# The first output projection of a two-layer attention kernel: ten of its sixteen strips in five pairs, each pair as seven block products

## What is computed

```python
o_mla = _mla_branch(...) * jax.nn.silu(gate_mla)     # 512 x 1024
o_fox = _fox_branch(...) * jax.nn.silu(gate_fox)     # 512 x 1024
o = jnp.concatenate([o_mla, o_fox], axis=-1) @ w_out # 512 x 2048 times 2048 x 2048
return x + _rms_norm(o, g_post)                      # what the second layer reads
```

## Time and profile before

| | |
|---|---|
| median of 3 runs | 1803.67 us |
| the profiled execution | 1803.62 us, its span 1801.8 us |
| PE busy | 1785.9 us, 99% of the span |
| DVE busy | 1043.7 us, 58% |
| ACT busy | 663.2 us, 37% |
| chain that ended last | 93% on PE |

### The profile page before, as it was taken

One profiled execution on the slowest core, in us unless ns is written; L12 is line 12 of the kernel. 1 busy time (PEld: TensorE's weight loads), 2 busy tenths in 40 slices (PEclk: granted clock), 3 DMA queues, 4 the chain that ended last, 5 costly groups with the idle time before them and its releaser, 6 DMA issues.

```text
span 1801.8 us, 24913 instructions
## 1 busy us (share of the span) xinstructions
PE 1785.9 (99%) x8748; PEld 1493.7 (83%) x8748; DVE 1043.7 (58%) x2150; ACT 663.2 (37%) x1265; POOL 49.0 (3%) x77
## 2 busy tenths in 40 slices
PE   9999999999999999999999999999999999999997
PEld 7788888888888888888878887888888888888887
DVE  7444434444433788853348865767667666784334
ACT  6433223222223444542236343434443334352222
POOL 0000000000000000000002000000000000000001
PEclk9999999999999999999999999999999999999999
DMA  6443434342232433233238364211212222223332
GB/s 238 141 124 116 130 102 119 111 120 85 85 102 71 139 106 128 94 113 102 94 97 225 105 220 142 70 58 59 81 47 83 84 68 81 75 77 129 116 122 100
DMA packets 56323, 196.46 MB, mean 109 GB/s; under 512 B 6624, under 2 KB 7800, under 8 KB 55744
## 3 DMA queue, kind: packets, MB, share of 16 engines
q1 hardware_dynamic: 49392, 170.87, 28.8%
q0 software_dynamic: 6864, 24.69, 5.3%
HBM read 187.11 MB, written 8.43 MB: 109 GB/s over the span
## 4 chain that ended last, share of the span: by engine, by line
PE 93%; DVE 4%; DVEq 1%; ACT 1%; issue 1%; DMA 0%; SPq 0%; ACTq 0%
PE strip L442 23%; PE strip L444 23%; PE strip L443 23%; PE scores L442 3%; PE scores L443 3%; PE scores L444 3%; PE outputs L444 2%; PE outputs L443 2%; PE outputs L442 2%; PE scores L484 1%; PE scores L536 1%; PE scores L544 1%; PE scores L943 1%; PE scores L540 1%; PE scores L966 1%; PE scores L902 1%
## 5 line engine op out<-in xcount | busy, mean ns | idle before, releaser
L442 PE MATMUL strip<-xh,wh 128*128 128x512 f32 (+1 forms) x1896 | 743.6, 392 | 2.5 <-DVE xl L1941 1.5
L444 PE MATMUL strip<-xh,wl 128*128 128x512 f32 (+1 forms) x1896 | 735.4, 388 | 0.0
L443 PE MATMUL strip<-xl,wh 128*128 128x512 f32 (+1 forms) x1896 | 734.8, 388 | 0.0
L1540 DVE TENSOR_TENSOR wl<-raw,wh 128x1024 fp32r<-128x1024 f32 (+3 forms) x306 | 354.7, 1176 | 141.9 <-ACT wh L1054 141.2
L442 PEld LDWEIGHTS strip<-xh,wh 128*128 128x128 f32 x1896 | 356.2, 188 | 77.3 <-DVE xl L1941 2.4
L444 PEld LDWEIGHTS strip<-xh,wl 128*128 128x128 f32 x1896 | 356.0, 188 | 74.0
L443 PEld LDWEIGHTS strip<-xl,wh 128*128 128x128 f32 x1896 | 356.4, 188 | 70.6 <-issue 0.5
L1054 ACT ACTIVATE wh<-raw 128x1024 fp32r<-128x1024 f32 (+3 forms) x308 | 305.8, 1018 | 130.7 <-PE strip L444 93.2
L1076 ACT ACTIVATE prob<-prob,nms 128x128 f32<-128x128 f32 (+3 forms) x128 | 70.3, 551 | 100.7 <-DVE nms L1595 100.7
L1326 ACT ACTIVATE e_t<-o 128x512 f32 (+1 forms) x29 | 18.3, 632 | 214.3 <-DVE o L2020 109.6
L1548 DVE TENSOR_TENSOR y<-strip,rb 128x512 f32<-128x512 f32 x47 | 32.5, 691 | 103.9 <-PE strip L444 101.7
(11 more groups left out here) (438 smaller groups left out, 2083.5 us busy)
## 6 DMA issues: line engine op xcount, KB each, us to landing
raw<-in_w SPq DMA_DIRECT2D x308, 512.0 KB, 3.5
mfox<-in_mfox POOLq DMA_DIRECT2D x8, 640.0 KB, 4.1
mfox<-decay POOLq DMA_DIRECT2D x8, 640.0 KB, 7.6
xn<-o POOLq DMA_DIRECT2D x4, 1024.0 KB, 8.0
xr<-xn POOLq DMA_DIRECT2D x16, 256.0 KB, 3.0
o<-in_xt SPq DMA_DIRECT2D x7, 512.0 KB, 9.3
out<-oh SPq DMA_DIRECT2D x14, 256.0 KB, 2.5
o<-in_xt POOLq DMA_DIRECT2D x13, 256.0 KB, 6.6
```

What stands on the lines that cost most here:

```text
L442: pe.matmul(out, ah, bh, start=first, stop=False, skip_group_check=shared)
L443: pe.matmul(out, ah, bl, start=False, stop=False, skip_group_check=shared)
L444: return pe.matmul(out, al, bh, start=False, stop=last, skip_group_check=shared)
L1540: v_.tensor_tensor(wl[s][:, :cols], raw[s][:, :cols], wh[s][:, :cols].bitcast(F32), ALU.subtract)\
```

## The change

Ten strips (6 to 15) become five pairs. A pair is a 2x2 block problem: two output strips (j, j+1) by two halves of the tokens, and each block sums over two halves of the 16 tiles. In place of 8 block products there are 7 (Winograd's form of Strassen's scheme). Each is 8 tiles x 3 matmuls of 256 columns. Four of them take sums of weight units, four take sums of activations.

Of the four units of a pair m0, m1 (strip j) and m2, m3 (strip j+1) VectorE makes four sums of 128x1024 in order: s1 = m2+m3, s2 = m0-m2, s3 = s1-m0, s4 = m1-s3. Products 0 to 6 use m0, s1, s3, m1, s2, s4, m3; each of the seven gets its `wh` on ScalarE and its `wl` on VectorE. The sums of activations are the same for all pairs: before the first pair VectorE makes three differences of 256 columns for each of 8 k and a fourth in place in `o` (`t_of`), ScalarE rounds them (`th`, 128x768), VectorE makes their remainders (`t_rest`), and the fourth is split in two instructions of 128x1024 on each engine (`last_tile`, `last_rest`).

The products go to three banks, of which each pair uses the other three: 0 and 3 to `bx`, 1 and 5 to `bz`, 2, 4 and 6 to `by`. What a bank holds in between is read out: `p1` by ScalarE, and `p15`, `p16` and three of the four quarters of the result by VectorE (256 columns each), the fourth by ScalarE. TensorE waits for `p1` ahead of product 3, for `p16` ahead of product 4, for the late half of strip j+1 ahead of product 6. The weights in HBM are the same, and four units are loaded for a pair. The loads and the memset of GpSimd move to the end of the last pair, and one unit's remainder of the next stage moves behind its fourth new tile.

```diff
+PAIRS = 5
+FEWER = 4 * PAIRS
...
-U_CMPIN = U_OUT1 + 32
+U_PAIRS = U_OUT1 + 12
+U_CMPIN = U_PAIRS + 8 * 5
...
+def conv(q, i=0):
+    return U_PAIRS + 8 * q + i
+def pair_unit(q, m):
+    return U_PAIRS + 4 * q + m
...
+    chunks = [at["rb"] + 6144 * i for i in (0, 2, 3, 4)] + [stage + 6144 * i for i in range(4)]
+    th = [place(f"th{i}", [P, 3, 256], F32R, chunks[i]) for i in range(8)]
+    tl = [place(f"tl{i}", [P, 3, 256], F32R, chunks[i] + 3072) for i in range(8)]
+    tf = [place(f"tf{i}", [P, 3, 256], offset=chunks[i] + 3072) for i in range(8)]
+    wsum = place("wsum", [P, 1024], offset=stage + 24576)
+    p1 = place("p1", [P, 256], offset=at["gate"])
+    p16 = place("p16", [P, 256], offset=at["gate"] + 1024)
+    p15 = place("p15", [P, 256], offset=at["rb"] + 30720)
...
+    def pair_banks(q):
+        return (sb[0], sb[1], sb[2]) if q % 2 == 0 else (pj[N_OUT1 % 2], pj[1 - N_OUT1 % 2], po)
+    pair_from = (raw[2], wsum, raw[2], raw[3], raw[0], wsum, raw[1])
...
+        for q_ in range(1, PAIRS):
+            for m in range(4):
+                u = pair_unit(q_, m)
+                sp.wait_ge(w_lo, conv(q_ - 1, (4, 4, 5, 8)[m]))
+                sp.dma_start(raw[u % SLOTS][:, :], d["w"][u, :, :]).then_inc(raw_full[u % SLOTS], 16)
...
-        g.wait_ge(o_done, 16)
-        g.memset(blk[:, :, :], 0.0).then_inc(blk_zero, 1)
+        g.wait_ge(w_used, conv(PAIRS - 1, 5))
         g.dma_start(xr1[:, :, :], d["xt"][:, 0:2, :]).then_inc(xr1_in, 16)
         g.dma_start(xr1c[:, :, :], d["xt"][:, 2:3, :]).then_inc(xr1c_in, 16)
         g.dma_start(cos2[:, :], d["cos_a"]).then_inc(tab2_in, 16)
         g.dma_start(sin2[:, :], d["sin_a"]).then_inc(tab2_in, 16)
+        g.wait_ge(w_used, conv(PAIRS - 1, 6))
+        g.memset(blk[:, :, :], 0.0).then_inc(blk_zero, 1)
...
-        with pe.Fori(1, KT // 2 - 1) as i:
-            for s in range(4):
-                half(pe, At(U_OUT1 + 4 + s, i, 4), N_OUT1 + s // 2, s % 2, N_OUT1 + 1 + s // 2 + i * 2)
+        for s in range(4):
+            half(pe, At(U_OUT1 + 8 + s), N_OUT1 + s // 2, s % 2, N_OUT1 + 1 + s // 2)
+        def product(q, i, out, first, bh, bl):
+            pe.wait_ge(w_lo, conv(q, 8 if i == 6 else i + 1))
+            slot = conv(q, i) % SLOTS
+            for k_ in range(8):
+                cols = slice(P * k_, P * k_ + P)
+                ins = three(pe, out[:, 0:256], wh[slot][:, cols], wl[slot][:, cols], bh(k_), bl(k_),
+                            first and k_ == 0, k_ == 7, True)
+            ins.then_inc(w_used, 2 if i == 6 else 1)
+        def of_x(first, tokens):
+            return lambda k_: xh[:, first + k_, tokens], lambda k_: xl[:, first + k_, tokens]
+        def of_t(j):
+            return lambda k_: th[k_][:, j, :], lambda k_: tl[k_][:, j, :]
+        for q_ in range(PAIRS):
+            bx, bz, by = pair_banks(q_)
+            pe.wait_ge(y_done, N_OUT1 + 2 * q_ + 4)
+            product(q_, 0, bx, True, *of_x(0, TOKENS[0]))
+            if q_ == 0:
+                pe.wait_ge(t_lo, 8)
+            product(q_, 1, bz, True, *of_t(0))
+            product(q_, 2, by, True, *of_t(1))
+            pe.wait_ge(p1_out, q_ + 1)
+            product(q_, 3, bx, False, *of_x(8, TOKENS[0]))
+            pe.wait_ge(w_part, 3 * q_ + 2)
+            product(q_, 4, by, False, *of_t(2))
+            product(q_, 5, bz, False, *of_x(8, TOKENS[1]))
+            pe.wait_ge(w_part, 3 * q_ + 3)
+            if q_ == 0:
+                pe.wait_ge(t4_lo, 2)
+            product(q_, 6, by, False, *of_x(0, TOKENS[1]))
...
+        def pair_hi(q, i):
+            if q == PAIRS:
+                act_hi(a, At(U_CMPIN + i))
                 return
-            a.wait_ge(acc_ready, 3)
-            a.wait_ge(w_used, U_CMPIN)
-            a.activation(e_t[:, :], pj[1 - N_OUT1 % 2][:, :], ACT.Square).then_inc(ev_act, 1)
-
-        two_strips(At(U_CMPIN - 4), last_square, more=(6,))
+            if i in (0, 3, 6):
+                u = pair_unit(q, {0: 0, 3: 1, 6: 3}[i])
+                a.wait_ge(raw_full[u % SLOTS], (u // SLOTS + 1) * 16)
+            else:
+                a.wait_ge(s_made, 4 * q + {1: 1, 4: 2, 2: 3, 5: 4}[i])
+            a.wait_ge(w_used, conv(q, i - 3))
+            a.activation(wh[conv(q, i) % SLOTS][:, :], pair_from[i][:, :], ACT.Copy).then_inc(w_hi, 2 if i == 6 else 1)
+        def last_tile(b):
+            a.wait_ge(w_used, U_PAIRS)
+            a.activation(xh[:, 4 * b:4 * b + 4, TOKENS[1]], o[:, 8 + 4 * b:12 + 4 * b, TOKENS[0]], ACT.Copy)\
+             .then_inc(t4_hi, 1)
...
+        for i in range(3):
+            pair_hi(0, i)
+        square_of(5)
+        for q_ in range(PAIRS):
+            bx, _, _ = pair_banks(q_)
+            j = 6 + 2 * q_
+            pair_hi(q_, 3)
+            if q_ == 0:
+                last_tile(0)
+            else:
+                square_of(j - 2)
+            a.wait_ge(w_used, conv(q_, 1))
+            a.wait_ge(y_done, N_OUT1 + j)
+            a.activation(p1[:, :], bx[:, 0:256], ACT.Copy).then_inc(p1_out, 1)
+            pair_hi(q_, 4)
+            if q_ == 0:
+                last_tile(1)
+            else:
+                a.wait_ge(r_done, N_OUT1 + j - 1)
+                square_of(j - 1)
+            pair_hi(q_, 5)
+            pair_hi(q_, 6)
+            a.wait_ge(w_used, conv(q_, 4))
+            a.activation(o[:, j, TOKENS[0]], bx[:, 0:256], ACT.Copy)
+            for i in range(3 if q_ < PAIRS - 1 else 2):
+                pair_hi(q_ + 1, i)
+        a.drain()
+        square_of(KT - 2)
+        a.wait_ge(r_done, N_OUT1 + KT - 1)
+        a.activation(e_t[:, TOKENS[1]], o[:, KT - 1, TOKENS[1]], ACT.Square)
+        a.wait_ge(y_done, N_OUT1 + KT)
+        a.activation(e_t[:, TOKENS[0]], o[:, KT - 1, TOKENS[0]], ACT.Square).then_inc(ev_act, 1)
+        act_hi(a, At(U_CMPIN + 2))
...
+        def t_of(k_):
+            early, late = TOKENS
+            v_.tensor_tensor(tf[k_][:, 0, :], o[:, k_, late], o[:, k_, early], ALU.subtract)
+            v_.tensor_tensor(tf[k_][:, 2, :], o[:, 8 + k_, late], o[:, k_, late], ALU.subtract)
+            v_.drain()
+            v_.tensor_tensor(tf[k_][:, 1, :], o[:, 8 + k_, late], tf[k_][:, 0, :], ALU.subtract)
+            v_.drain()
+            v_.tensor_tensor(o[:, 8 + k_, early], o[:, 8 + k_, early], tf[k_][:, 1, :], ALU.subtract).then_inc(t_made, 1)
+        def t_rest(k_):
+            v_.wait_ge(t_hi, k_ + 1)
+            v_.tensor_tensor(tl[k_][:, :, :], tf[k_][:, :, :], th[k_][:, :, :].bitcast(F32), ALU.subtract)\
+              .then_inc(t_lo, 1)
...
+        def pair_lo(q, i):
+            if q == PAIRS:
+                lo(v_, At(U_CMPIN + i))
+                return
+            slot = conv(q, i) % SLOTS
+            v_.wait_ge(w_hi, conv(q, 8 if i == 6 else i + 1))
+            v_.tensor_tensor(wl[slot][:, :], pair_from[i][:, :], wh[slot][:, :].bitcast(F32), ALU.subtract)\
+              .then_inc(w_lo, 2 if i == 6 else 1)
+        def loaded(q, m):
+            u = pair_unit(q, m)
+            v_.wait_ge(raw_full[u % SLOTS], (u // SLOTS + 1) * 16)
+        def first_sums(q):
+            loaded(q, 2)
+            loaded(q, 3)
+            v_.tensor_tensor(wsum[:, :], raw[0][:, :], raw[1][:, :], ALU.add).then_inc(s_made, 1)
+            loaded(q, 0)
+            v_.tensor_tensor(raw[0][:, :], raw[2][:, :], raw[0][:, :], ALU.subtract).then_inc(s_made, 1)
+        def third_sum(q):
+            v_.drain()
+            v_.tensor_tensor(raw[2][:, :], wsum[:, :], raw[2][:, :], ALU.subtract).then_inc(s_made, 1)
+        def fourth_sum(q):
+            v_.drain()
+            loaded(q, 1)
+            v_.tensor_tensor(wsum[:, :], raw[3][:, :], raw[2][:, :], ALU.subtract).then_inc(s_made, 1)
+        t_of(0)
+        t_of(1)
...
+        out1(4)
+        out1_square(4)
+        t_rest(7)
+        pair_lo(0, 0)
+        first_sums(0)
+        pair_lo(0, 1)
+        third_sum(0)
+        pair_lo(0, 2)
+        fourth_sum(0)
+        out1(5)
+        out1_square(5)
+        for q_ in range(PAIRS):
+            bx, bz, by = pair_banks(q_)
+            j = 6 + 2 * q_
+            more = q_ < PAIRS - 1
+            pair_lo(q_, 3)
+            if q_ == 0:
+                last_rest(0)
+            pair_lo(q_, 4)
+            if q_ == 0:
+                last_rest(1)
+            else:
+                out1_square(j - 2)
+            v_.wait_ge(p1_out, q_ + 1)
+            v_.wait_ge(w_used, conv(q_, 2))
+            v_.tensor_tensor(p15[:, :], bz[:, 0:256], p1[:, :], ALU.add).then_inc(w_part, 1)
+            pair_lo(q_, 5)
+            if q_ > 0:
+                out1_square(j - 1)
+            v_.wait_ge(w_used, conv(q_, 3))
+            v_.tensor_tensor(p16[:, :], by[:, 0:256], p1[:, :], ALU.add).then_inc(w_part, 1)
+            pair_lo(q_, 6)
+            if more:
+                pair_lo(q_ + 1, 0)
+            v_.drain()
+            v_.wait_ge(w_used, conv(q_, 5))
```

(23 more changed lines are left out.)

130 lines of the change are left out of this document (92 added, 38 removed).

## The result

| | before | after |
|---|---|---|
| median | 1803.73 us (15 runs, 1803.16 to 1804.07) | 1807.02 us (15 runs, 1805.80 to 1808.63) |
| ratio after / before | | 1.0019, 95% interval 1.0012 to 1.0026 |
| the profiled execution | 1803.62, span 1801.8 | 1806.3, span 1804.5 |

The change costs 3.3 us, 0.19%. That is inside the range and within 0.2% of the forecast, but the forecast was +0.8. The five pairs save nothing, as predicted; some 2.5 us come on top.

What follows compares the result with a forecast made beforehand. The prediction took a VectorE-ScalarE chain of waits to bound the pairs, giving back TensorE's saving of 1.6 us a pair. Pairs end +0.26, the work behind them makes +0.77: 1803.62 + 0.77 = 1804.4 us, range 1800 to 1810.

Steps and rivals of the forecast that it cites:

- The loop binds, not TensorE: In the pairs, a VectorE-ScalarE chain from product 4 to the next pair's product 4 sets the pace; chance 0.60.
- TensorE binds: Rival in the pairs: chain 2 us shorter than read, only product 6 waits, 1797.3 us in all; chance 0.12.
- Paces: TensorE in the pairs: 256-column matmuls 0.1198 us each, a product 2.88; VectorE sums priced like remainders, 1.22, 1.14 in a run.
- The period: From product 4 of one pair to that of the next: 22.2 us, against 21.76 for a pair before.
- VectorE's margin of 0.2: Ahead of the first product 4: `p16` ready at 836.35, wanted at 836.62, after VectorE works almost without rest for 56 us.
- dearer hand-overs: Rival in the loop: hand-overs or drains cost 0.1 us more at nine places, 1808 us; chance 0.14.
- The tail: Behind the pairs: last product ends +0.26 us; `acc` and squares queue behind next-stage work, so the feature sums start +0.77.
- From there on all is as before: After the feature sums behind the pairs, nothing more is lost or gained; the total stays +0.77 us.
- The moved remainder: Next stage, behind its fourth new tile: delays VectorE by 1.14 us, hidden, so no cost; 1 us at most otherwise.
- The clock: Rival in the pairs: 1.6 us pauses halve TensorE's clock, product 4 takes up to twice 2.88, 1816 us; chance 0.04.
- Late m3: Rival in the loop: m3's load exceeds 4.67 us and delays the first sum; at 6.5 us, 1811.7 in all; chance 0.10.
- The weighed rule: VectorE in the loop: no operation starts before the previous leaves its pipe; three places would cost 0.08 more each, 1 us.

Runs made afterwards that it cites:

- the exchanges: Changed kernel with product 5's `wh` ahead of the square's wait on ScalarE, product 6's read-out ahead of the next pair's first `wl` on VectorE: both 1798.48 us.
- the added sum: Changed kernel with one more 128x1024 VectorE sum in pairs 0 to 3, behind the next pair's first `wl`: 1811.24 us; ahead of it: 1806.70 us.
- making the unit early: Changed kernel with the second layer's unit 3 copied and its remainder made at the end of the pairs: 1807.02 us; with both exchanges too: 1799.12 us.

## Why the prediction was right, and what it missed

- **The loop binds, not TensorE: right, and shown.** Product 4 waits for `p16` in pairs 1 to 4, from start to start by 1.8 (predicted 1.6; the 1.65 of the bracket is another measure, and that it looks closer is chance), product 6 by 0.26 (0.2; 886.55 to 886.93 for a pace of 0.12), VectorE's longest idle time is 3.23 (3) ahead of lo 0 and ended by ScalarE, and it is busy 15.90 of 22 us (17). The proof is in the exchanges and the added sum, not in the waits. The rival "TensorE binds" was put at a chain 2 us shorter, and both exchanges made one 1.9 shorter: 5.0 us under before, where the rival said 6.3.
- **Paces.** Product 0 of pair 0 starts 43.52 behind strip 2, as predicted; the pace of 256 columns held. The sums cost as the remainders (1.22, 1.14 in a run), which the prediction had taken.
- **The period: 22.36 for 22.23.** The term was mis-sized by 0.13, out of hand-overs that are each a little dearer; the largest is `p1`, which starts 0.09 after the read-out for 0.04. The first loop missed by 0.24, since product 4 of pair 0 already has a restart that I had left out (0.39 for 0.28). And that product starts 0.16 later than forecast, 0.05 behind `p16`: VectorE's margin of 0.2 in the 56 us ahead of the pairs was used up. In all (0.16 + 0.24 + 3 x 0.13) the last product ends 0.8 later than forecast. In size this is a fifth of the rival "dearer hand-overs"; in kind, only part of it is hand-overs.
- **The tail: +1.66 at L681 for +0.77.** 0.77 of the 0.89 missed is that of the pairs. The rest, 0.12, is that `acc` is now what TensorE waits for (0.43 ahead of L677).
- **"From there on all is as before": the step that failed.** It is where the most is missing. The prediction put it at nothing; the two profiles of the changed kernel have 1.2 and 1.1 more from L681 to the sums of squares (47.68 and 47.61 for 46.47). VectorE's 0.34 at one place of its code is inside the norm, which the prediction held to be unchanged: the work was, its place in the code was not. The prediction had named the pairs' written-out code and counted nothing for it, by a row of TensorE; the 0.34 arose on VectorE. In four profiles of its variants half a clock costs another 0.7 there.
- **The moved remainder: the cover was read at the wrong reader.** The prediction looked at tile 5 (ready 954.44, read 957.27), which held. The reader that matters is `pe_sum`, which waits for `acc` at the end of the same VectorE work, with 1.32 to spare less 0.19 for the hand-over, not 2.8. "It would cost 1 us at most" held, but by luck: the waits of 0.62 and 0.66 in the profiles are half the unit's and half a slower load's, and the medians show no gain from making the unit early.
- **The clock: a rival at the wrong place.** It was to fall in the pairs, ahead of product 4; the windows of all profiles have 1.00 there, with pauses of 1.65 in 22.36. It falls behind the last pair, in four profiles of twelve, at a small part of the price.
- **Late m3 did not happen.** No idle time ahead of s1 ends on a transfer, and the period repeats to 0.01 us over two profiles.
- **The weighed rule.** The Trainium skill (VectorE: DVE Perf Modes, The DRAIN you can't avoid) has an operation wait until the one in front has left its pipe, and adds that a next operation which is not held starts earlier; the prediction left the addition out and worked out 1 us. The trace of after has the addition's case: s1 and s2 take 1.22 and start 1.13 apart (886.79, 887.92).

So the 3.3 us are 1.0 from the pairs, 0.6 from the hand-over behind them and 0.35 at one place of VectorE's code, all seen in both profiles of the changed kernel; and about 1.3 whose cause stays open. For this the profiles show pieces, a wait of 0.6 to 0.7 at the sums of squares or 0.7 of half a clock, and 0.4 to 0.5 between the sums of squares and the end. How large each is in the median isn't settled.

## What to carry to other kernels

An engine that is busy for two thirds of the time can set the pace: walk the loop of waits once around, and count its length, not its work. Of each link ask whether it must stand in that order; here two exchanges of neighbours in the order, one on each of two engines, turned +3.3 us into -5.0, and one more sum costs 4.5 us or nothing, by whether it stands behind or ahead of one instruction. When work is moved under cover, look up every reader behind it in that engine's order, down to the last, and price the cover by the one with the least to spare.
